# Linear attention's inner levels with unpadded queries, dot products moved behind the last projection block, and a changed end of the kernel

## The reference, cut to what matters

```python
def step(state, inp):                      # gla_chunked, chunks of 64 tokens
    qi, ki, vi, gi = inp
    b = jnp.cumsum(gi, axis=2)
    o_inter = jnp.einsum('bhtk,bhkv->bhtv', qi * jnp.exp(b), state)
    diff = b[:, :, :, None, :] - b[:, :, None, :, :]
    decay = jnp.exp(jnp.where(causal, diff, -jnp.inf))
    scores = jnp.einsum('bhtk,bhsk,bhtsk->bhts', qi, ki, decay)
    o_intra = jnp.einsum('bhts,bhsv->bhtv', scores, vi)
    ...
o_g = rms_norm(o_g, gla_out_norm[i]).reshape(B, S, GLA_WIDTH) * jax.nn.silu(g_r)
...
x = x + _rmsnorm(ff, g_mlp_post[l])        # the last line of the second block
```

## Time and profile before

| | |
|---|---|
| median of 3 runs | 2545.72 us (2540.93 to 2549.39) |
| the profiled execution's own time | 2545.55 us |
| its span, first to last instruction | 2543.9 us |
| mean granted TensorE clock | 0.983 |
| PE busy | 2445.4 us (96%) |
| DVE busy | 1710.9 us (67%) |
| ACT busy | 1061.1 us (42%) |

### The profile page before, as it was taken

The page is one execution under the profiler, slowest core; times in us unless marked ns, Lnnn a source line. Parts: engine busy times, 40 slices in busy tenths (PEclk is TensorE's granted clock), DMA queues, the critical chain, the costliest instruction groups (busy, mean ns, idle before and its releaser), DMA issues.

```text
span 2543.9 us, 29142 instructions
## 1 busy us (share of the span) xinstructions
PE 2445.4 (96%) x11190; PEld 1938.6 (76%) x11190; DVE 1710.9 (67%) x2077; ACT 1061.1 (42%) x1497; POOL 129.4 (5%) x216
## 2 busy tenths in 40 slices
PE   8998789999999999999999999999999999999995
PEld 6777655578888887878788777778778888878784
DVE  5237877644877778788873555345478877786888
ACT  5225476634433333333542233343355433334335
POOL 1001000000000010000001000000001000100001
PEclk9998899999999999999999999999999999999997
DMA  6110000033333372600134111124435433615103
GB/s 220 42 42 21 1 1 1 18 119 129 133 119 114 100 255 109 215 17 17 42 99 151 42 66 67 67 100 149 149 125 197 142 128 105 226 52 205 47 1 132
DMA packets 76163, 252.11 MB, mean 99 GB/s; under 512 B 6273, under 2 KB 6305, under 8 KB 76001
## 3 DMA queue, kind: packets, MB, share of 16 engines
q1 hardware_dynamic: 43776, 131.08, 15.8%
q0 software_dynamic: 32256, 119.27, 12.5%
HBM read 186.76 MB, written 62.91 MB: 98 GB/s over the span
## 4 chain that ended last, share of the span: by engine, by line
PE 82%; DVE 10%; issue 5%; ACT 3%; DMA 0%; POOL 0%; DVEq 0%; SPq 0%; ACTq 0%; POOLq 0%
PE ps L2577 29%; PE ps L2909 19%; PE ps L2947 19%; PE ps L3075 6%; PE ps L3003 1%; PE ps L2842 1%; PE ps L3021 1%; DVE opQ_lo L2021 1%; PE ps L2872 1%; DVE opQ_lo L2024 1%; PE ps L2793 1%; PE ps L2852 1%; PE ps L3012 1%; DVE opP_lo L1547 1%; DVE X L2075 1%
## 5 line engine op out<-in xcount | busy, mean ns | idle before, releaser
L2947 PE MATMUL ps<-opQ_hi 128*128 128x512 f32 x896 | 349.9, 391 | 6.1 <-DVE opQ_lo L2024 6.1
L2947 PE MATMUL ps<-opQ_lo,opQ_hi 128*128 128x512 f32 x896 | 348.7, 389 | 0.0
L2947 PE MATMUL ps<-opQ_hi,opQ_lo 128*128 128x512 f32 x896 | 348.6, 389 | 0.0
L2947 PEld LDWEIGHTS ps<-opQ_hi 128*128 128x128 f32 x896 | 168.2, 188 | 44.6 <-DVE opQ_lo L2024 7.0
L2577 PE MATMUL ps<-opP_hi,w_hi 128*128 128x512 f32 x640 | 199.9, 393 | 2.4 <-ACT Z L1090 1.1
L2577 PE MATMUL ps<-opP_lo,w_hi 128*128 128x512 f32 x640 | 198.1, 391 | 0.0
L2577 PE MATMUL ps<-opP_hi,w_lo 128*128 128x512 f32 x640 | 197.5, 390 | 0.0
L2947 PEld LDWEIGHTS ps<-opQ_hi,opQ_lo 128*128 128x128 f32 x896 | 168.2, 188 | 35.1
L2947 PEld LDWEIGHTS ps<-opQ_lo,opQ_hi 128*128 128x128 f32 x896 | 168.2, 188 | 34.8 <-issue 0.2
L816 ACT ACTIVATE w_hi<-w_stage 128x1024 fp32r<-128x1024 f32 x104 | 109.2, 1050 | 172.7 <-PE ps L2577 149.8
L1208 ACT ACTIVATE opQ_hi<-spot 128x1024 fp32r<-128x1024 f32 x80 | 84.9, 1061 | 229.8 <-PE ps L2947 190.8
(11 more groups left out here) (414 smaller groups left out, 4801.8 us busy)
## 6 DMA issues: line engine op xcount, KB each, us to landing
w_stage<-in_w_stream SPq DMA_DIRECT2D x104, 512.0 KB, 3.6
h_spill<-T POOLq DMA_DIRECT2D x56, 512.0 KB, 5.0
pair_raw<-in_w_stream SPq DMA_DIRECT2D x26, 1024.0 KB, 5.8
spot<-in_w_stream SPq DMA_DIRECT2D x24, 1024.0 KB, 7.2
spot<-h_spill POOLq DMA_DIRECT2D x24, 1024.0 KB, 9.2
qh_raw<-in_w_stream SPq DMA_DIRECT2D x8, 1024.0 KB, 11.2
ql_raw<-h_spill POOLq DMA_DIRECT2D x8, 1024.0 KB, 8.3
g_spill<-T POOLq DMA_DIRECT2D x16, 512.0 KB, 2.9
```

The lines of the kernel that those rows point to most:

```text
L2947: mm = pe.matmul(ps[:, down_bank(sc, f) + m, :], weight, operand, start=(g == 0 and kt == 0 and weight is wh and operand is hi), stop=(g = ...
```

## The change: what it does

1. **Unpadded queries.** For levels 2 to 5, and for QX, the queries are written without zeros, [partition, 512] a pair and level and [partition, 1024] for QX: one DVE instruction over 128 partitions instead of two over 64. Each product on PE becomes two with 64 rows and 64 columns, one for each head, whose results go to two PSUM banks. Level 1 stays padded. The memsets of QX go, that of QE[1] is split by pair.
2. **Dot products.** QK is made before the evacuation of block 15 (in KE[1], once the low part of block 15 is made) and summed behind block 15, ahead of `block_scores(0)`, into bank 1. ACT does `level(2)` first, then copies the sums, then writes all of the diagonal of pair 0. Step 2's factors, which overwrite KE[1], wait for the sums.
3. **Evacuations.** The heads' outputs lie one head to two whole banks, so that ACT reads rows of 1024 in one run (L1000, L1002), and merges read one bank a head.
4. **Order in the latent attention.** A one-column Ln stands before `keys_out(7)`, `root_log` is split around `queries_out(7)`; `root_inverse` goes from units 1, 3, 5, 7 to 6, 8, 10, 12, `gla_out` from 3 to 10 to 8 to 15, the high parts from 8, 10, 12, 14 to 24, 26, 28, 30, the low parts from 9, 11, 13, 15 to 25, 27, 29, 31.
5. **The end.** The folds come before the first `end_scale(1, ...)`; the four sums of squares of tiles 4 to 7 of half 0 go from DVE to PE (matmuls with ones that accumulate); for two of the eight pairs the residual is added on PE by products with the identity and copied back by ACT (`pair_out`); five instead of two gains of half 1 come early; the last add and the last store are split in two.

```diff
+        def right_queries(lv, pr):
+            return QE[lv % 2][:, pr, 0:4, :, :].rearrange("p w b t -> p (w b t)")
...
-            pool.memset(QX[:, 0, :, :, :], 0.0).then_inc(g["zero"], 1)
-            pool.memset(QE[1][:, :, :, :, :], 0.0).then_inc(g["zero"], 1)
-            pool.memset(QX[:, 1, :, :, :], 0.0).then_inc(g["zero"], 1)
+            for pr in range(2):
+                pool.memset(QE[1][:, pr, :, :, :], 0.0).then_inc(g["zero"], 1)
...
             act.wait_ge(mm_done, B_WOUT)
+            level(2)
+            act.wait_ge(g["dot"], DOT + 1)
+            act.activation(dots, ps[:, 1, 0:32], ACT.Copy).then_inc(g["diag"], 1)
...
-            diagonal(0, range(0, 2))
-            level(2)
-            diagonal(0, range(2, WIN)).then_inc(g["diag"], 1)
+            diagonal(0, range(WIN)).then_inc(g["diag"], 1)
...
+            act.activation(small[:, 46:47], one_c, ACT.Ln)
             keys_out(7)
+            root_log(2)
             queries_out(7)
-            root_log()
+            root_log(3)
...
+            def pair_out(j):
+                act.wait_ge(n4["stat"], 3 + j + 1)
+                act.activation(end_pair(X, 1, j), banks(2 + 2 * j, 2).rearrange("p (m t) -> p m t", t=HALF), ACT.Copy)\
+                   .then_inc(n4["ln"], 1)
...
             for o in range(DT):
                 end_gain(0, o)
+                if o in (1, 5):
+                    pair_out(o // 4)
...
                 if lv >= 2:
                     v.wait_ge(g["lmm"], level_mm_no(earlier(n, 2)))
-                for par in range(2):
-                    r = slice(64 * par, 64 * par + 64)
...
+                    ins = v.scalar_tensor_tensor(right_queries(lv, pr).rearrange("p (n l) -> p n l", l=size), halves(q_t[:, pr, :]), GDK ** -0.5,
+                                           halves(EX[lv % 2][:, pr, :]), ALU.mult, ALU.mult)
...
             exponents(3)
             exponents(8)
+            v.wait_ge(w_lo_done, B_WIN + 16)
+            v.tensor_tensor(QK[:, :, :], q_t, k_t, ALU.mult).then_inc(g["qk"], 1)
             win_step(B_WIN + 15, None, 15, 1, False)
...
+                v.scalar_tensor_tensor(QX[:, pr, :, :].rearrange("p c t -> p (c t)"), q_t[:, pr, :], GDK ** -0.5, EB[:, pr, :],
+                                       ALU.mult, ALU.mult).then_inc(g["qx"], 1)
...
-                if 3 <= u < 11:
-                    gla_out(u - 3)
-                if u in (9, 11, 13, 15):
-                    k = (u - 9) // 2
+                if 8 <= u < 16:
+                    gla_out(u - 8)
+                if u in (25, 27, 29, 31):
+                    k = (u - 25) // 2
...
-            end_scale(1, 0)
             for o in range(4):
                 last_fold(1, o)
-            for o in range(4, DT):
-                end_add(0, o)
-            for j in range(1, 4):
+            for j in range(4):
                 end_scale(1, j)
...
-                    key = k_t[:, pr, w * P:(w + 1) * P] if lv == LAST_LEVEL else KE[lv % 2][:, pr, w * P:(w + 1) * P]
-                    mm = pe.matmul(banks(level_bank(n), 2)[:, w * P:(w + 1) * P], key, QE[lv % 2][:, pr, w, :, :], start=True, stop=True)
+                    for par in range(2):
+                        r = slice(64 * par, 64 * par + 64)
+                        key = k_t[r, pr, w * P:(w + 1) * P] if lv == LAST_LEVEL else KE[lv % 2][r, pr, w * P:(w + 1) * P]
+                        mm = pe.matmul(ps[:, level_bank(n) + par, w * CHUNK:(w + 1) * CHUNK], key,
+                                       right_queries(lv, pr)[r, w * CHUNK:(w + 1) * CHUNK], start=True, stop=True)
...
                 for c in chunks:
-                    pe.matmul(banks(4, 4)[:, c * P:(c + 1) * P], ST8[:, pr, c, :], QX[:, pr, c, :, :], start=(c % 4 == 0), stop=False)
+                    for par in range(2):
+                        r = slice(64 * par, 64 * par + 64)
+                        pe.matmul(head_bank(par)[:, c * CHUNK:(c + 1) * CHUNK], ST8[r, pr, c, :], QX[r, pr, c, :],
+                                  start=(c % 8 == 0), stop=False)
...
-            half_statistic(n5, 2, 1, res_sum)
+            pe.wait_ge(n5["sum"], 2 * DT + 4)
+            pe.matmul(ps[:, 1, :], ones[:, :], res_sum[:, :], start=True, stop=False)
+            for o in range(4, DT):
+                pe.wait_ge(n5["sq"], 2 * DT + o + 1)
+                mm = pe.matmul(ps[:, 1, :], ones[:, :], end_sq[(o - 1) % 4], start=False, stop=(o == DT - 1))
+            mm.then_inc(n5["stat"], 1)
+            for j in range(2):
+                a, m0 = j // 2, 2 * (j % 2)
+                pe.wait_ge(n4["scaled"], 2 * DT + j + 1)
+                for x in range(2):
...
+                    for tiles in (X, Xend):
+                        mm = pe.matmul(ps[:, 2 + 2 * j + x, :], ident[:, :], end_pair(tiles, 1, j)[:, x],
+                                       start=(tiles is X), stop=(tiles is Xend))
```

More of the change, by code:

```diff
@@ L187, in build @@
         decay = small[:, 8:40]
-        QK = at("QK", [P, 2, S], XB)
+        QK = KE[1]
         head_pick = small[:, 3:5]
@@ L796, in _ @@
                 pool.dma_start(Xend[:, k, :], t["x_spill"][k * P:(k + 1) * P, :]).then_inc(tile_landed[k], 16)
-            for j in range(4):
-                pool.wait_ge(n4["added"], 2 * DT + j + 1)
+            for j in range(2, 4):
+                pool.wait_ge(n4["added"], 2 * DT + j - 1)
+                pool.dma_start(out_pair(1, j), end_pair(X, 1, j)).then_inc(ya_stored, 16)
+            for j in range(2):
+                pool.wait_ge(n4["ln"], 3 + j + 1)
                 pool.dma_start(out_pair(1, j), end_pair(X, 1, j)).then_inc(ya_stored, 16)
@@ L926, in _ @@
             act.activation(rot[:, :, :, :].rearrange("p a b c -> p (a b c)"), ps[:, 6, 256:320], ACT.Copy).then_inc(mha["krc"], 1)
-            act.wait_ge(g["dot"], DOT + 1)
-            act.activation(dots, ps[:, 6, 320:352], ACT.Copy).then_inc(g["diag"], 1)
             for w in range(WIN):
@@ L1017, in roots_raw, with root_log @@
                     act.activation(head_root[h], banks(2 * h, 2), ACT.Copy).then_inc(g["ln"], 1)
-            def root_log():
+            def root_log(h):
                 act.wait_ge(g["ln"], GH)
-                for h in range(2, GH):
-                    act.activation(head_root[h], head_root[h], ACT.Ln, scale=1.0 / GDV, bias=eps_c).then_inc(g["ln"], 1)
+                act.activation(head_root[h], head_root[h], ACT.Ln, scale=1.0 / GDV, bias=eps_c).then_inc(g["ln"], 1)
             def root_inverse(h):
@@ L1515, in _ @@
             half_root(n4, 2, 0, end_r[1])
-            for o in range(2, DT):
-                end_gain(1, o)
             for o in range(4, DT):
                 end_square(0, o)
+            for o in range(5, DT):
+                end_gain(1, o)
             half_root(n5, 2, 1, end_r[0])
@@ L2546, in end_scale @@
                 v.wait_ge(n4["scaled"], 2 * DT + 4 * (1 - h) + j + 1)
-                for m in range(m0, m0 + 2):
-                    v.wait_ge(tile_landed[2 * m + a], END_BACK[2 * m + a])
-                v.tensor_tensor(end_pair(X, h, j), end_pair(X, h, j), end_pair(Xend, h, j), ALU.add).then_inc(n4["added"], 1)
+                if h == 0 or j >= 2:
+                    for m in range(m0, m0 + 2):
+                        v.wait_ge(tile_landed[2 * m + a], END_BACK[2 * m + a])
+                    if h == 0 and j == 3:
+                        for x in range(2):
+                            v.tensor_tensor(end_pair(X, h, j)[:, x], end_pair(X, h, j)[:, x], end_pair(Xend, h, j)[:, x], ALU.add)\
+                             .then_inc(n4["added"], 1)
+                    else:
+                        v.tensor_tensor(end_pair(X, h, j), end_pair(X, h, j), end_pair(Xend, h, j), ALU.add).then_inc(n4["added"], 1)
             for o in range(4, DT):
@@ L2654, in _ @@
             pe.wait_ge(evac_done, B_WIN + 12)
-            pe.wait_ge(g["qk"], QK_MADE + 1)
-            pe.wait_ge(ones_set, 6)
-            for pr in range(2):
-                for w in range(WIN):
-                    i = 2 * (pr * WIN + w)
-                    mm = pe.matmul(ps[:, 6, 320 + i:322 + i], QK[:, pr, w * P:(w + 1) * P], head_pick, start=True, stop=True)
-            mm.then_inc(g["dot"], 1)
             for w in range(WIN):
@@ L2755, in _ @@
             pe.wait_ge(g["trc"], WIN + 4)
+            pe.wait_ge(g["qk"], QK_MADE + 1)
+            pe.wait_ge(ones_set, 6)
+            pe.wait_ge(evac_done, B_WIN + 15)
+            for pr in range(2):
+                for w in range(WIN):
+                    i = 2 * (pr * WIN + w)
+                    mm = pe.matmul(ps[:, 1, i:i + 2], QK[:, pr, w * P:(w + 1) * P], head_pick, start=True, stop=True)
+            mm.then_inc(g["dot"], 1)
             block_scores(0)
```

75 lines of the change are left out of this document (38 added, 37 removed).

## The result

The changed kernel takes 2525.72 us (median of 4 runs, 2522.78 to 2525.88), the kernel before in the same comparison 2544.69 us (2540.93 to 2549.39): a ratio of 0.9922, 95% interval 0.9903 to 0.994, so 0.6 to 1.0% faster. The forecast was 2529. Sum and sign came out nearly right, its terms did not all: between the two traces the linear attention gave 4.7 us of the 8.5 forecast, and the softmax units, forecast at nothing, gave 5.8. That misses on both sides cancel is luck, as far as the sum goes.

What follows compares the result with a forecast made beforehand. PE holds 82% of the chain, so edits count only where DVE or ACT keeps it waiting. 2545.55 - 8.5 (parts 1 and 2) - 2.4 (part 3) - 0 (part 4) - 5.7 (part 5) = 2528.95, so 2529 us; 8 in 10: 2520 to 2540.

Steps and rivals of the forecast that it cites:

- The tie behind block 15: Linear attention: the new wait for the sums ends 3.6 us after block 15, level with DVE's 3.5 us of other work.
- I take no difference from 2.05: Inner levels on PE: a step of 32 half-size instructions costs the old 2.05 us, in a range of 1.8 to 3.6.
- loads one after the other: Rival, chance 0.12: row halves load in turn, inner steps cost 3.6 us instead of 2.05; 2540 us, no measurable change.
- DVE's saving of 0.69 us each: Levels 2 to 5: one DVE instruction over 128 partitions instead of two over 64 saves 0.69 us in each step.
- the 5.2 us of DVE: Up to 277.59 us PE waits for DVE's merges, so four steps and both `inter_queries` give 5.2 us there.
- Two signs that the forecast had named against itself: Inner levels: step times near 3.6 us, or DVE waiting for PE between steps 3 and 6, would show the prediction wrong.
- if `queries_out(7)` is delayed by all of that, 2.0: Ahead of the first exponential: the table change gains 2.0 us instead of 2.4 if the early Ln work delays `queries_out(7)`.
- the second pair's share of the work: Softmax units 16 to 31: the second pair of heads pays 3.6 us for its share of the finishing work.
- the price in the wide units: Softmax units: moved work costs 12.0 us there: `gla_out` 6.0, low parts 3.6, high parts 2.4.
- The rival of gaps in the wide units: Rival, chance 0.10: DVE work moved there makes PE rest and its clock fall; 0.05 near 2542 us, 0.05 beyond 2553.
- DVE's 5.8: The end: folds, sums and residual adds save DVE 6.6 us, less 0.8 of new waiting, so 5.8 remain.
- that rival: Rival, chance 0.08: PE's clock falls to its lower level before the end's identity products; the end gives nothing, 2535 us.

Runs made afterwards that it cites:

- second trace of before: The kernel before, unchanged, profiled a second time: 2546.61 us in that execution, against 2545.55 in its first.
- halves in turn: The changed kernel with all products of the first head, on rows 0 to 63, ahead of all of the second, not alternating: 2562.43 us in its profiled execution.

## Why the prediction was right, and where not

**Part 1, the dot products: right, 3.4 of 3.5, with 2.9 to 5.2 as the traces spread.** The tie behind block 15 was lost by 0.9 us (4.52 us for the sums instead of 3.63, in a stretch where the clock falls), and the state updates behind them take 1.5 more as well. Unforeseen was the other side: at the old place the transposes behind the same products take 0.9 to 2.4 us more, so that block 15 is 4.2 us sooner and not 3.5, and against the second trace of before the move is worth 6.8. The size is right partly because the two offset each other.

**Part 2, the unpadded queries: the term that was mis-sized, 1.3 (0.9 to 3.2) instead of 5.0.** The step "I take no difference from 2.05" was right for PE at its upper level (2.00), and "loads one after the other" was rightly held unlikely: that is what halves in turn show (3.55). DVE's saving of 0.69 us each came true too. Wrong was the silence on PE's clock between 242 and 287 us: the 5.2 us of DVE were taken as arriving because PE waited for DVE, but at half clock a level and an `inter_output` take 3.63 us each, and PE then sets the pace for 15 to 30 us. Two signs that the forecast had named against itself so came: three of the eight steps take 3.6 to 3.7 us, and between steps 3 and 6 DVE waits 1.54 and 1.15 us for PE. With padded products PE was at 0.84. Shown is that it goes with the form of the products: in 257 to 272 us all ten runs with 64-row products have 0.50 to 0.52 with PE busy 13.0 to 13.9 us, the two with 128-row ones behind moved dot products 0.84 with 8.0 and 8.3, the two of the kernel before 0.77 with 9.7. Why the chip grants less there isn't shown; the busy time is in part the effect, as the same work takes nearly twice as long. The rival "loads one after the other" counted on a PE that never rests to keep the upper clock; with the halves in turn PE is busy 13.45 of 15 us in 272 to 287 and stays at 0.50.

The page "TensorEngine Tiling (Array Packing)", section "Key Properties", of the Trainium skill, by which different tiles load and multiply in parallel, agrees with these runs for 64x128 tiles, 2.00 against 3.55 us, with the bank order left open as said above.

**Part 3, the table: right, 2.1 of 2.4.** The forecast's note "if `queries_out(7)` is delayed by all of that, 2.0" is what happened: 0.3 us.

**Part 4, the order: forecast 0 within 4, worth 2.2.** The traces show 5.8, but 3.2 of them are that execution's own, most of them in units 16 to 31, where its clock was 0.81 for 18 us. The forecast read the 3.6 us between 40.55 and 36.96 as the second pair's share of the work; but only two low parts, at 406.33 and 409.59, lie behind unit 15's exponential, and the second trace has 38.00 us there, 1.0 over its third pair. The term that was off besides is the price in the wide units: the splits alone stood at 3.6 + 2.4 = 6.0 us, but from unit 15 to unit 47 the new order takes 77.9 us and the old one 76.0, 1.9 more. There PE sets the pace (busy 19.39 of 20 us in 410 to 430), and most of the moved work fits beside it. The rival of gaps in the wide units fell with that.

**Part 5, the end: right, 5.0 of 5.7.** DVE's 5.8 came out at 5.74; the time from the last add to the end of the span was the term off, 0.66 instead of 0.1. PE kept its upper level (1.02 us a sum), so that rival fell.

**The balance.** 3.4 + 1.3 + 2.1 + 2.2 + 5.0 = 14.0 us for the change itself, against 16.6 forecast. So the forecast's 2529 came within 3.3 us of 2525.72 partly by luck: part 2 gave about 3.7 less than its term, part 4 gave 2.2 more, and 5 us that belong to no term made up the rest. The traces differ by 20.0, with 3.2 from the clock in the units, 0.4 more there, 0.4 at the start and 1.9 between the output projection and the mix statistic. Of that last, no edit lies there, and one run of changed code has 1981.98 like before, the others 1980.3 to 1980.7; its cause stays open. The medians of before and after are 19.0 apart, so 5 us of it are not put down to an edit: before's first trace was slow in the units, but its second lost as much at the dot products, and I can't say what a mean over many would give each part. By medians against the changed kernel's the order is 4.1, the padding 2.8 and the end 5.05 us; the intervals of the first two overlap the changed kernel's.

## What to carry to other kernels

Where one engine's work is cut, look at the clock that the next engine will have in the new rhythm, not only at its durations in the old trace: here most of the gain of VectorE met half speed on TensorE. Look also at what stands in the queue behind products with few columns to a load: here it was slower at both places, the transposes before and the state updates after. And before a trace's difference is put down to an edit, profile the same kernel twice: 3 us in two places were the execution's own.

## What the hardware showed that I had not expected

- TensorE can be busy 41.5 of 43 us from 257 to 300 us and stay at 0.50 all the while, and the same program can return to 1.00 at 272 us in another execution. Of six timed runs two were 11 to 14 us longer.
- 32 products of two columns take 3.6 to 4.6 us, and 28 transposes behind them 4.55, 4.95 and 6.01 us in three executions instead of 3.66.
- Products of 64 rows and 64 columns that alternate between the row halves cost 62 ns each at the upper level, 113 ns at the lower; the same ones in turn 111 and 197 ns.
- With a last store of 256 KB the span ends 3.84 us behind the last add; with one of 512 KB, and more time between stores, it ended 3.18 behind it.
